# Moving a mixture-of-experts layer's weights in pairs of ring slots, from a layout with 16 KB rows

## What is computed

```python
def expert_choice_ffn(h, w_router, w_gate, w_up, w_down):
    aff = jax.nn.softmax(jnp.einsum('bsd,de->bse', h, w_router), axis=-1)
    g, idx = lax.top_k(aff.transpose(0, 2, 1), cap)          # cap = 64, 16 experts
    xe = h[bidx, idx]
    hid = (jax.nn.silu(jnp.einsum('becd,edf->becf', xe, w_gate))
           * jnp.einsum('becd,edf->becf', xe, w_up))         # d = 1024, f = 2048
    ye = jnp.einsum('becf,efd->becd', hid, w_down) * g[..., None]
    return jnp.zeros_like(h).at[bidx, idx].add(ye)
```

## Time and profile before

| | |
|---|---|
| time, median of 3 runs | 2097.74 us (2092.34 to 2097.86) |
| the profiled execution | 2091.48 us, of which the span of its instructions is 2089.4 us |
| granted TensorE clock, mean | 0.99 |
| PE busy | 1934.3 us, 93% of the span |
| DVE, ACT, POOL busy | 725.9, 523.4, 80.5 us |
| DMA | 505.37 MB in 100012 packets |

### The profile page before, as it was taken

The page is one execution under the profiler, slowest core; times in us unless marked ns, Lnnn a source line. Parts: engine busy times, 40 slices in busy tenths (PEclk is TensorE's granted clock), DMA queues, the critical chain, the costliest instruction groups (busy, mean ns, idle before and its releaser), DMA issues.

```text
span 2089.4 us, 20846 instructions
## 1 busy us (share of the span) xinstructions
PE 1934.3 (93%) x8754; PEld 1146.5 (55%) x8754; DVE 725.9 (35%) x1121; ACT 523.4 (25%) x816; POOL 80.5 (4%) x67
## 2 busy tenths in 40 slices
PE   7999999999999899899986999988888898888897
PEld 6777788888877777677863333322222232222232
DVE  6534544333456775666443111101111111011111
ACT  4443422322245442456622000000000000000001
POOL 2000000000014401000000000000000000000000
PEclk9999999999999999999998999999999999999999
DMA  4221133233323222212554999999999999999996
GB/s 164 89 91 51 61 131 101 93 100 100 103 81 111 91 80 73 91 61 65 193 217 159 419 418 416 417 416 416 418 419 419 416 416 417 417 417 419 418 417 276
DMA packets 100012, 505.37 MB, mean 242 GB/s; under 512 B 10240, under 2 KB 10752, under 8 KB 66768
## 3 DMA queue, kind: packets, MB, share of 16 engines
q1 hardware_dynamic: 99600, 503.88, 61.4%
q10 hardware_dynamic: 320, 0.17, 0.0%
HBM read 499.82 MB, written 4.19 MB: 241 GB/s over the span
## 4 chain that ended last, share of the span: by engine, by line
PE 62%; DMA 28%; DVE 4%; ACT 3%; SPq 1%; issue 1%; POOL 1%; ACTq 0%; DVEq 0%; POOLq 0%
PE ps L1784 37%; DMA ring_a<-in_w_up_e 10%; PE ps L2102 9%; DMA ring_a<-in_w_gate_e 7%; DMA ring_b<-in_w_up_e 6%; DMA ring_b<-in_w_gate_e 4%; PE ps L2113 3%; PE ps L1743 3%; PE ps L2085 2%; SPq L610 1%; PE ps L2063 1%; PE ps L1958 1%; PE ps L1835 1%; PE ps L1832 1%; PE ps L1934 1%
## 5 line engine op out<-in xcount | busy, mean ns | idle before, releaser
L2102 PE MATMUL ps<-ring_a,xe 128*64 128x512 f32 x1376 | 318.2, 599 | 50.6 <-DMA ring_a<-in_w_up_e 35.2
L1102 DVE TENSOR_TENSOR d_lo<-d_raw,d_hi 128x1024 fp32r<-128x1024 f32 x168 | 210.6, 1263 | 113.8 <-ACT d_hi L735 113.3
L2102 PEld LDWEIGHTS ps<-ring_a,xe 128*64 128x64 f32 x1376 | 90.9, 136 | 275.4 <-issue 165.2
L2102 PE MATMUL ps<-ring_b,xe 128*64 128x512 f32 x672 | 156.8, 600 | 28.2 <-DMA ring_b<-in_w_up_e 20.4
L1291 DVE TENSOR_TENSOR hid<-sg,ps 128x512 f32<-128x512 f32 x32 | 20.6, 684 | 466.2 <-PE ps L2102 466.2
L1784 PE MATMUL ps<-n_hi,d_hi 128*128 128x512 f32 x448 | 175.6, 392 | 1.5 <-DVE d_lo L1102 0.8
L735 ACT ACTIVATE d_hi<-d_raw 128x1024 fp32r<-128x1024 f32 x168 | 173.0, 1049 | 10.2 <-DMA d_raw<-in_tiles_in 9.5
L1784 PE MATMUL ps<-n_hi,d_lo 128*128 128x512 f32 x448 | 174.5, 389 | 0.0
L1784 PE MATMUL ps<-n_lo,d_hi 128*128 128x512 f32 x448 | 174.4, 389 | 0.0
L1665 DVE TENSOR_TENSOR x<-x,ps 128x1024 f32<-128x1024 f32 x60 | 69.2, 1215 | 271.6 <-PE ps L2085 271.6
L2113 PE MATMUL ps<-ring_a,hidT 128*64 128x512 f32 x688 | 156.1, 597 | 6.1 <-ACT hidT L1080 3.9
(11 more groups left out here) (421 smaller groups left out, 2684.3 us busy)
## 6 DMA issues: line engine op xcount, KB each, us to landing
ring_a<-in_w_gate_e SPq DMA_DIRECT2D x88, 1024.0 KB, 20.9
ring_a<-in_w_down_e SPq DMA_DIRECT2D x86, 1024.0 KB, 23.2
d_raw<-in_tiles_in SPq DMA_DIRECT2D x168, 512.0 KB, 3.4
ring_a<-in_w_up_e SPq DMA_DIRECT2D x84, 1024.0 KB, 27.1
ring_b<-in_w_up_e SPq DMA_DIRECT2D x44, 1024.0 KB, 27.0
ring_b<-in_w_down_e SPq DMA_DIRECT2D x42, 1024.0 KB, 23.3
ring_b<-in_w_gate_e SPq DMA_DIRECT2D x40, 1024.0 KB, 21.1
x_in<-in_xT_in SPq DMA_DIRECT2D x4, 512.0 KB, 6.6
```

The costliest lines, as they stand in the source:

```text
L1102: dve.tensor_tensor(d_lo[:, n % SLOTS, :, :], d_raw[:, n % SLOTS, :, :], d_hi[:, n % SLOTS, :, :].bitcast(F32), ALU.subtract).then_inc(t_l ...
L2102: mm = pe.matmul(ps[half * CAP:(half + 1) * CAP, 2 * m + q, :], xe[:, k, :], slot(e, n)[:, (2 * q + half) * S:(2 * q + half + 1) * S], sta ...
```

## The change

The host writes all expert weights into one array `experts_in` of 192 blocks. A block is two neighbouring slots (g even, g + 1) side by side: for each of the 128 partitions the row of slot g and behind it that of slot g + 1, 16 KB in one piece. For the down matrix the four rows of 4 KB that a partition gets from two slots lie in one piece too. What each slot holds in SBUF is the same as before.

The transfers are listed in MOVES: slots 0 to 5 alone, then pairs (6, 7), (8, 9) up to (378, 379), then slots 380 to 383 alone, 197 moves in place of 384. A pair fills two neighbouring places of the ring with one DMA. A move of a single slot takes its 8 KB half of the 16 KB rows. `load_weights` waits until the last slot that the move overwrites has been used, so for a pair until two slots are free. The semaphores go round by the move, `s_ring[m % RING]`, and TensorE waits, ahead of each slot, for the move that brings it. When the moves are sent within the dense stage is as before: slots 0 to 4 between the tiles, 5 to 11 behind them, 12 to 17 after the last group.

```diff
+ALONE, TAIL = 6, 4
+MOVES = [(g, 1) for g in range(ALONE)] + [(g, 2) for g in range(ALONE, NE * PER - TAIL, 2)]
+MOVES += [(g, 1) for g in range(NE * PER - TAIL, NE * PER)]
+MOVE_OF = [m for m, (g, n) in enumerate(MOVES) for _ in range(n)]
...
-        gate_v = w_gate_e_2[0].rearrange("e (k p) f -> p e k f", p=P)
-        up_v = w_up_e_2[0].rearrange("e (k p) f -> p e k f", p=P)
-        down_v = w_down_e_2[0].rearrange("e (c j p) d -> p e c j d", p=P, j=2)
...
         def slot(e, n):
-            s = (e * PER + n) % RING
-            return ring_a[:, s, :] if s < RING_A else ring_b[:, s - RING_A, :]
+            return slots(e * PER + n, 1)
+
+        def slots(g, n):
+            s = g % RING
+            rows = ring_a[:, s:s + n, :] if s < RING_A else ring_b[:, s - RING_A:s - RING_A + n, :]
+            return rows.rearrange("p s f -> p (s f)")
...
-            def load_expert(e, first=0, last=PER):
-                for n in range(first, last):
-                    g = e * PER + n
-                    src = gate_v[:, e, n, :] if n < 8 else up_v[:, e, n - 8, :] if n < 16 else down_v[:, e, n - 16, :, :]
-                    dst = slot(e, n) if n < 16 else slot(e, n).rearrange("p (j d) -> p j d", j=2)
-                    if g >= RING:
-                        sp.wait_ge(s_used, g - RING + 1)
-                    sp.dma_start(dst, src).then_inc(s_ring[g % RING], 16)
+            def load_weights(first, last):
+                for m in range(first, last):
+                    g, n = MOVES[m]
+                    if g + n > RING:
+                        sp.wait_ge(s_used, g + n - RING)
+                    sp.dma_start(slots(g, n), experts_in[g // 2, :, g % 2 * FF:(g % 2 + n) * FF]).then_inc(s_ring[m % RING], 16)
...
-                    load_expert(0, STREAM[FIRST[n]].i, STREAM[FIRST[n]].i + 1)
+                    load_weights(STREAM[FIRST[n]].i, STREAM[FIRST[n]].i + 1)
                 load1(n)
             sp.wait_ge(mb_dve.sem, mb_dve.count("lo", 7))
-            load_expert(0, 5, RING_A)
+            load_weights(5, MOVE_OF[RING_A])
             stage_done(sp, "out2", 7)
-            load_expert(0, first=RING_A)
-            for e in range(1, NE):
-                load_expert(e)
+            load_weights(MOVE_OF[RING_A], len(MOVES))
...
             def chunk(e, n):
-                g = e * PER + n
-                pe.wait_ge(s_ring[g % RING], (g // RING + 1) * 16)
+                m = MOVE_OF[e * PER + n]
+                pe.wait_ge(s_ring[m % RING], (m // RING + 1) * 16)
...
+    def experts():
+
+        both = np.empty((NE, PER // 2, P, 2, FF), np.float32)
+        for n, w in enumerate(("w_gate_e_2", "w_up_e_2")):
+            both[:, 4 * n:4 * n + 4] = inputs[w][0].reshape(NE, 4, 2, P, FF).transpose(0, 1, 3, 2, 4)
+        both[:, 8:] = inputs["w_down_e_2"][0].reshape(NE, 4, 4, P, D).transpose(0, 1, 3, 2, 4).reshape(NE, 4, P, 2, FF)
+        return both.reshape(NE * PER // 2, P, 2 * FF)
```

More of the change, by code:

```diff
@@ L227, in kernel_program @@
 def kernel_program(nc, xT_in, pT_in, table, gla_mask_in, rstm_in, negm_in, selr_in, m01_in, dist_in, tiles_in,
-                   w_gk2, diff_lam_2, w_router_2, w_gate_e_2, w_up_e_2, w_down_e_2, norm_f_g_2, x3_store, out):
+                   w_gk2, diff_lam_2, w_router_2, experts_in, norm_f_g_2, x3_store, out):
     ctx = ExitStack()
@@ L2242 @@
         "tiles_in": np.stack([packed(tile) for tile in TILES]),
+        "experts_in": experts(),
     }
-    for name in ("w_gk2", "diff_lam_2", "w_router_2", "w_gate_e_2", "w_up_e_2", "w_down_e_2",
-                 "norm_f_g_2"):
+    for name in ("w_gk2", "diff_lam_2", "w_router_2", "norm_f_g_2"):
         feed[name] = inputs[name]
```

## The result

The changed kernel takes 2074.68 us (median of 4 runs, 2071.27 to 2078.86) against 2095.54 us (median of 4, 2092.34 to 2097.86): a ratio of 0.9903 with an interval of 0.9882 to 0.9924. That is 1.0% faster, some 21 us, and outside the 0.3% that a measurement of this kernel can leave in doubt. 2080.3 was forecast, with a range of 2070 to 2091. In the profiled executions the span went from 2089.4 to 2072.6 us; 2072.0 was forecast.

The account below looks back on a forecast made before the run. The prediction took the experts' weight transfers as the bound, with PE covered. Longer rows -20.9, release in pairs +1.73 and landing in pairs +1.73 gave -17.4 us, from the median 2097.7 to 2080.3 us, range 2070 to 2091.

Parts of the forecast that it names:

- What bounds it: Expert stage: weight transfers set the time, an expert fed in 60.2 us while PE needs 51.2, leaving 9 us of cover.
- The packet price: Weight transfers: each row is a packet costing 8.8 ns on its engine beside its bytes; longer rows save 20.9 us.
- The two pair savings of the forecast: Expert weight transfers: 16 KB rows save 0.070 us per gate or up pair and 0.211 us per down pair.
- The 9 us of ramp and late landings: Gapless stretch: 9 us beyond the summed transfer times, from first transfers' ramp and some late landings, taken as unchanged.
- Half as many DMAs: Weight transfers: 179 fewer completion packets on each engine, worth 0 to 1.6 us, taken as 0.
- Release and landing in pairs: Waiting for two slots at the stage's start and for the partner at the last up slot, 1.73 us lost each.
- The Trainium skill's packet rule: Weight transfers: about 3 cycles, 3.5 ns, a packet; the rows would then bring 8.3 us, the kernel 2092.9 us.
- Rival A: Down slots: slow from two rows 512 KB apart, not packets; gain only 8.3 us less 3.46, 2092.9 us; chance 0.11.
- Rival B: Weight transfers: long rows hinder each other in memory; 2118 us if pairs went at today's slowest rate; chance 0.08.
- C: Weight transfers: more gain than expected, 16 KB rows at 434 GB/s, giving 2067.9 us; chance 0.09.

Follow-up runs that it names:

- e3: New host order by slots, but every slot moved alone as 256 rows of 4 KB, a partition's two rows 512 KB apart; 2112.57 us.
- e4: The changed kernel's pairs, each moved as 512 rows of 4 KB lying 4.25 KB apart in a padded source; 2114.42 us.
- e1: The changed kernel's new order of slots, but every slot moved alone in rows of 8 KB, 384 DMAs; 2086.13 us, ratio 0.9958.
- e2: The changed kernel's pairs and 197 DMAs, but each pair carried as 256 rows of 8 KB; 2088.5 us.
- e10: The changed kernel with slots in threes, rows of 24 KB, and slots 0-5, 18-23 and 372-383 alone; 2069.97 us, ratio 0.9885.
- e7: The changed kernel with only slots 374 and 375 moved alone too; 2072.72 us, stage 929.24 us.
- e6: The changed kernel with only slots 18 to 21 moved alone too; 2078.05 us, stage 930.11 us.
- e11: The changed kernel with slots 18 to 21, 374 and 375 moved alone too; 2071.07 us, ratio 0.9892, stage 927.8 us.
- e9: The changed kernel run again, unaltered, as partner on one chip; 2074.89 us, ratio 0.9909, stage 930.7 us.
- e8: The changed kernel with SP waiting from slot 18 on as if the ring had 12 slots; 2085.35 us, stage 941.58 us.

## Why the prediction was right

**What bounds it** held: the changed kernel's middle is DMA all through, at 428 GB/s as forecast, and PE's longer pauses in the middle cost nothing.

**The packet price** held from 4 to 24 KB. Each trace also keeps the semaphore counts of every DMA, the last of which is its landing. The table gives the time for 2 MiB in two ways: from PE's rows in the gate phase (the middle one of the experts in 1290 us to the end), and as the median distance of landings in 1290 to 2020 us:

| rows | packets an engine | DMA of | PE's rows, gate phase | landings |
|---|---|---|---|---|
| 4 KB (e3, e4) | 32 | 1 MiB; 2 MiB | 5.10; 5.11 | 5.12; 5.12 |
| 8 KB (e1, e2) | 16 | 1 MiB; 2 MiB | 4.956; 4.957 | 4.970; 4.970 |
| 16 KB (changed) | 8 | 2 MiB | 4.881 | 4.894 |
| 24 KB (e10) | 5.3 | 3 MiB | 4.87 | 4.869 |

By the landings, 32 to 16 packets is 0.150 us, 9.4 ns each, 16 to 8 is 0.076 us, 9.5 ns each, and 8 to 5.3 is 0.025 us, 9.4 ns each: the price is linear up to 24 KB. PE's rows come out 0.01 to 0.02 us lower for 4 to 16 KB and with nearly the same differences, because in the changed kernel, as before, the first gate matmul starts 0.13 us after its landing and the last up matmuls 0.04 to 0.05 us. In e10 that first matmul mostly doesn't wait at all, so its 4.87 must not be held against 4.881.

The forecast had 8.8 ns. Its 2.485 us for a slot with 8 KB rows is what e1's landings show too. Its 2.555 us for one with 4 KB rows, read from eight slots of one expert, is 2.560 in e3, and 0.005 us over 8 packets is the difference. The two pair savings of the forecast, 0.070 and 0.211 us, came out at 4.957 - 4.881 = 0.076 and ((23.02 - 2.48) - (24.57 - 4.88)) / 4 = 0.21 us, where 23.02 and 24.57 us are the middle times from a last up slot to the next first gate slot or pair. 120 x 0.076 + 59 x 0.21 = 21.5 us, and 21.7 were found. The 9 us of ramp and late landings that the forecast took as unchanged were so: 179 x 4.894 = 876.0 leaves 9.1 of the 885.1 us.

**Half as many DMAs**, bounded at 0 to 1.6 us and taken at 0, is 0 within what the traces show (e1 against e2: 0.001 us a pair).

**Release and landing in pairs**, 1.73 us each, were seen at 1.72 and 1.71 in the marks. e2 against e1 shows them paid in full, 1.72 at the start and 1.74 at the end, with 898.3 and 898.4 us between. Taking them back in the changed kernel brings less: at the end all but 0.2 us (e7), at the start 0.6 (e6) to 1.5 us (e11 against e7).

**The Trainium skill's packet rule** (DMA: Bandwidth & Descriptors, "Why small descriptors are slow"), about 3 cycles, 3.5 ns by the forecast's estimate, gave 2092.9 us; the measurement decides for 9.4 ns on this path. The same page's fixed 2 us for a DMA, which it fits on GpSimd's path while SP issues here, don't add up when DMAs are queued: e1 against e2.

**Rival A** fell with the changed kernel's gate phase, which had no distant rows to cure and yet gained 0.076 us, and with e4. **Rival B** fell: 16 KB rows ran at 428 GB/s, and 24 KB rows at 430. **C**, 434 GB/s from a window of 5 us, was too good: the forecast had called such short windows good to a per cent at best.

The difference of the medians, 20.9 us, is 3.5 us more than forecast, while that of the spans, 16.8 us, is 0.6 less. The marks say why the second is the one to judge the working by: before the stage begins the executions differ by 1.5 us and more, and the granted clock in the dense stage and in the pauses of the routing differs between them too. The forecast time of 2080.3 us is 5.6 us too long. Of these 2.2 come from its base, the median of three runs (2097.74; with a fourth it is 2095.54), and 3.5 from the medians' difference, which the packets do not explain. Neither belongs to the mechanism, and neither is more than one execution differs from another by.

**The late landings.** In every trace some experts take 0.3 to 1.6 us longer. Between 1379.74 and 1971.50 us ten experts of the changed kernel take 59.18 us on average where most take 58.7 to 59.1, and before it was 60.67, most 60.2. Neither row length nor DMA size took it away. The traces hold the cause. The same DMA engines also carry a queue that the profile calls instruction; in 1150 to 2030 us of the changed kernel it has

```profile
q8 instruction: 29, 0.48, 0.2%
```

29 packets of 16 KB, one every 30 us. A DMA has landed with the last of 16 counts, one for each engine. In e9 one such packet begins at 1400.3 us. Up to the landing before it the last count comes 0.23 us behind the next to last; from the landing at 1402.9 us on it is 1.79 us. One engine was held up by 1.55 us and stays behind, and as it was already the last one, every later landing moves with it. PE's rows show it at the first gate pair, beside that of the next expert:

```profile
1403.07 2.44 PE L2103 MATMUL ps<-ring_b,xe 128*64 128x512 f32 x8 [2.49 <-DMA ring_b<-in_experts_in]
...
1461.79 1.94 PE L2103 MATMUL ps<-ring_a,xe 128*64 128x512 f32 x8 [0.94 <-DMA ring_a<-in_experts_in]
```

A packet at 1371.4 us delayed an engine that was 2.0 us ahead of the last, and no landing moved. In the thirteen traces together 52 landings between 1290 and 2020 us came over 0.4 us later than usual, and each had an instruction packet in the 8 us before it, though there is one only every 30 us. In e9, as in the kernel before, there are three such landings, so they are no part of what the change gained. What decides which engine such a packet meets is not shown.

## What to carry to other kernels

When a queue of large DMAs never runs dry, look at the length of one contiguous row, not at the size or number of the DMAs: on this path each packet had a fixed price of 9.4 ns on its engine, which is 6% of a 4 KB row, 3% of an 8 KB row and 1.5% of one of 16 KB. Coarser moves are paid for at the two ends of the gapless stretch, where the first buffer is released and where the last data are waited for, so move single pieces there. And where a few microseconds in two thousand count, date the stage from marks in the trace, since the stages around it wander by as much.

## What the runs showed of the hardware

- A packet of 4 to 24 KB costs 9.4 ns on its engine beside its bytes. Bytes alone cost 4.819 us for 2 MiB (4.894 less 8 packets of 9.4 ns), 435 GB/s on 16 engines; reached in the middle of the stage were 409 with 4 KB rows, 421 with 8 KB, 428 with 16 KB, 430 with 24 KB.
- The completion of a DMA costs nothing that shows when others are queued behind it: 2 MiB in rows of 8 KB take 4.970 us in one DMA or two (e2, e1).
- A 16 KB packet of the instruction queue holds one DMA engine up by 1.55 us, and landings wait for the engine that is furthest behind (e9).
- The rate is the same whether an issue lands after 25 us or 40 us (e8 4.883 us, changed kernel 4.884 us for a pair).
- TensorE kept its full granted clock (1.00) through pauses of 1.2 us every 4.9 us. With pauses of 1.94 us after each triple it ran some of the next matmuls at the lower level (24 matmuls in 7.07 us in place of 5.37, granted clock 0.76), not after each such pause.
